# The first expert's rows by a one-hot product instead of a gather, in a hybrid decoder layer with a mixture of experts

## The reference, cut to what matters

```python
h = rms_norm(x, norm_ffn[l]) * (1 + sc2) + sh2
x = x + g2 * hier_moe(h, ...)

def hier_moe(h, w_rg, b_rg, w_re, b_re, w_gate, w_up, w_down):
    ...
    for gi in range(N_EXPERT_GROUPS):
        hid = silu(einsum('nd,edf->nef', t, w_gate[gi])) * einsum('nd,edf->nef', t, w_up[gi])
        y = y + einsum('nef,efd->nd', hid * combine[:, gi, :, None], w_down[gi])
```

## Time and profile before

| | |
|---|---|
| Median of 3 runs | 785.83 us (782.81 to 786.27) |
| The profiled execution: own time, span of its trace | 787.4 us, 785.7 us |
| Mean granted TensorE clock | 0.941 of full speed |
| Busy in the span: PE, DVE, ACT, POOL | 681.1, 317.3, 180.1, 117.9 us |
| Moved by DMA | 174.13 MB, mean 222 GB/s |

### The profile page before, as it was taken

How to read it: one execution, slowest core, us unless ns; L and a number is a source line. 1 busy time by engine, 2 the same in 40 slices (tenths; PEclk the granted TensorE clock), 3 DMA queues, 4 the chain that set the end, 5 groups by cost and what they waited for, 6 DMA issues and landing times.

```text
span 785.7 us, 9804 instructions
## 1 busy us (share of the span) xinstructions
PE 681.1 (87%) x3799; PEld 396.2 (50%) x3803; DVE 317.3 (40%) x749; ACT 180.1 (23%) x434; POOL 117.9 (15%) x165
## 2 busy tenths in 40 slices
PE   1799999999999998889999953999999999999820
PEld 1674446667675796555544443444544544443300
DVE  3204757757576443766522245350211211212117
ACT  3205224031120212556511140120211211201103
POOL 8700124123050273000000001010000000000030
PEclk9999999999999999989999975899999999999975
DMA  9999003973330302640161077438999999999964
GB/s 329 375 261 362 2 0 108 300 236 108 108 108 1 55 2 104 181 201 1 67 202 54 28 304 311 161 105 357 370 424 411 403 410 407 390 406 414 415 205 181
DMA packets 73826, 174.13 MB, mean 222 GB/s; under 512 B 21970, under 2 KB 38956, under 8 KB 69932
## 3 DMA queue, kind: packets, MB, share of 16 engines
q1 hardware_dynamic: 67728, 157.59, 55.1%
q0 software_dynamic: 2816, 9.96, 3.6%
q10 hardware_dynamic: 3228, 5.84, 2.0%
HBM read 157.12 MB, written 16.26 MB: 221 GB/s over the span
## 4 chain that ended last, share of the span: by engine, by line
PE 74%; DVE 8%; DMA 7%; POOL 4%; ACT 3%; issue 3%; POOLq 0%; ACTq 0%; SPq 0%; DVEq 0%
PE ps L1025 14%; PE ps L1141 7%; PE ps L2281 7%; PE ps L1058 6%; PE ps L2248 5%; DMA gu<-in_w_up 4%; PE ps L1019 4%; PE ps L2359 2%; PE ps L2365 2%; PE ps L2245 2%; PE ps L1053 2%; PE ps L2272 2%; POOL lev L1629 2%; PE ps L653 2%; PE ps L2369 2%
## 5 line engine op out<-in xcount | busy, mean ns | idle before, releaser
L1025 PE MATMUL ps<-gu,xgT 128*128 128x512 f32 x256 | 114.1, 605 | 2.8 <-ACT xgT L1068 2.8
L1025 PEld LDWEIGHTS ps<-gu,xgT 128*128 128x128 f32 x256 | 49.1, 194 | 63.3 <-issue 63.3
L1521 POOL DMA_INDIRECT xg<-xn_rows,list x16 | 14.9, 930 | 390.7 <-PE ps L994 182.6
L2281 PE MATMUL ps<-hT,winr 128*128 128x512 f32 x144 | 72.6, 612 | 0.2
L1141 PE MATMUL ps<-wout,yT 128*128 128x512 f32 x128 | 57.6, 609 | 0.0
L1058 PE MATMUL ps<-dn,hidT 128*128 128x512 f32 x128 | 56.5, 594 | 0.0
L1734 POOL TENSOR_TENSOR cc<-low,lev 128x512 f32<-128x512 f32 x20 | 30.2, 1520 | 129.5 <-DVE low L2068 104.0
L1872 DVE SCALAR_TENSOR_TENSOR acc<-ada,st,acc 128x512 f32<-128x512 f32 x56 | 48.5, 867 | 1.3
L1019 PE MATMUL ps<-gu,xgT 128*32 128x256 f32 (+1 forms) x384 | 43.0, 452 | 1.1 <-DMA gu<-in_w_up 1.1
L2248 PE MATMUL ps<-hT,wind 128*128 128x512 f32 x96 | 42.3, 593 | 0.0
L1141 PEld LDWEIGHTS ps<-wout,yT 128*128 128x128 f32 x128 | 24.6, 195 | 30.0 <-issue 30.0
(11 more groups left out here) (429 smaller groups left out, 1041.4 us busy)
## 6 DMA issues: line engine op xcount, KB each, us to landing
dn<-in_w_down SPq DMA_DIRECT2D x16, 2048.0 KB, 23.5
gu<-in_w_gate SPq DMA_DIRECT2D x15, 2048.0 KB, 22.2
gu<-in_w_up SPq DMA_DIRECT2D x15, 2048.0 KB, 26.7
ada<-in_w_ada SPq DMA_DIRECT2D x12, 2048.0 KB, 11.7
expert_rows<-zero SPq DMA_DIRECT2D x12, 512.0 KB, 7.0
expert_rows<-yo ACTq DMA_DIRECT2D x8, 512.0 KB
wout<-in_w_out SPq DMA_DIRECT2D x1, 3072.0 KB, 10.4
x<-in_x SPq DMA_DIRECT2D x2, 1024.0 KB, 6.4
```

The lines of the kernel that those rows point to most:

```text
L1025: ins = nc.tensor.matmul(PS[2 * b + w][:, :], T["xgT"][:, k, :], w_in[:, w, k, :], start=(k == 0), stop=(k == KT - 1))
L2281: ins = t.matmul(bank[:, :], w(k), T["hT"][:, k, :], start=(k == 0), stop=(k == KT - 1))
```

## The change

Gather 0, its list and its transposes go. In their place PE multiplies x2 itself (stationary, 128 tokens x 128 features) with the one-hot matrix of expert 0 (moving, 128 tokens x 128 rows), summed over the four token tiles, for each of the eight feature steps: 32 matmuls whose results in PS[6] and PS[7] are already transposed rows. `rstd2` is folded into the one-hot matrix, which is now made by four instructions of 128 x 128 instead of one of 128 x 512. As the features are in the natural order now, the first expert's gate and up are loaded as `(k p) f -> p k f`, and its scale and shift are `A2` and `mod` directly. The waits of the later transposes for their gathers are counted one lower on the even tiles, which share `xg[0]`. The rank products move from PS[6] to PS[4]. ACT starts on its half after the fourth feature step (`first_half`). Expert 1's list product comes after the 32 matmuls on PE, and its copy (and so gather 1) behind `dve_rows(0)` on DVE.

```diff
+    first_v = [A[n][0].rearrange("g e (k p) f -> (g e) p k f", p=P)[0] for n in ("w_gate", "w_up")]
...
-        load_gate_up(sp, 0, 0)
+        for w, view in enumerate(first_v):
+            sp.dma_start(gu[0][:, w], view).then_inc(sem("gu_in0"), 16)
...
     def act_rows(act, n):
-        act.wait_ge(sem("mod_moved"), 48)
-        act.wait_ge(sem("xg_tr"), n + 1)
+        if n:
+            act.wait_ge(sem("mod_moved"), 48)
+            act.wait_ge(sem("xg_tr"), n + 1)
+        else:
+            act.wait_ge(sem("first_half"), 1)
+        scale, shift = (rA, rshift) if n else (A2, mod[:, 24:32])
...
-        rank = PS[6][:, 0:(ST + 1) * E]
+        rank = PS[4][:, 0:(ST + 1) * E]
...
-        for e in range(2):
-            pe.wait_ge(sem("routing"), ROUTING[("first_rows", "second_rows")[e]])
+        pe.wait_ge(sem("routing"), ROUTING["first_rows"])
+        for k in range(KT):
             for i in range(ST):
-                ins = t.matmul(PS[4 + e][:, 0:1], T["in_row"][:, e, i, :], T["tok"][:, i:i + 1], start=(i == 0),
-                               stop=(i == ST - 1))
-            ins.then_inc(sem("routing_pe"), 1)
-
-        pe_rows(pe, 0, 0, 16)
+                ins = t.matmul(PS[6 + k // 4][:, (k % 4) * P:(k % 4 + 1) * P], T["x2"][:, i, k * P:(k + 1) * P],
+                               T["in_row"][:, 0, i, :], start=(i == 0), stop=(i == ST - 1))
+            if k == 3:
+                ins.then_inc(sem("first_half"), 1)
+        ins.then_inc(sem("xg_tr"), 1)
+        pe.wait_ge(sem("routing"), ROUTING["second_rows"])
+        for i in range(ST):
+            ins = t.matmul(PS[5][:, 0:1], T["in_row"][:, 1, i, :], T["tok"][:, i:i + 1], start=(i == 0),
+                           stop=(i == ST - 1))
+        ins.then_inc(sem("routing_pe"), 1)
         pe_gate_up(pe, 0, 0)
...
-        for e in range(2):
-            v.scalar_tensor_tensor(T["in_row"][:, e], T["row_n"][:].unsqueeze(1).broadcast_to([P, ST, P]), 1.0,
-                                   r16[:, :, e:e + 1].broadcast_to([P, ST, P]), ALU.add,
-                                   ALU.is_equal).then_inc(sem("routing"), 1)
+        link(v.tensor_scalar(r16, r16, -1.0, None, ALU.add))
+        for i in range(ST):
+            ins = v.tensor_scalar(T["in_row"][:, 0, i, :], T["row_n"][:], r16[:, i, 0:1], rstd2[:, i:i + 1],
+                                  ALU.is_equal, ALU.mult)
+        ins.then_inc(sem("routing"), 1)
+        v.tensor_tensor(T["in_row"][:, 1], T["row_n"][:].unsqueeze(1).broadcast_to([P, ST, P]),
+                        r16[:, :, 1:2].broadcast_to([P, ST, P]), ALU.is_equal).then_inc(sem("routing"), 1)
...
-        dve.wait_ge(sem("routing_pe"), ROUTING_PE["first_list_mm"])
-        v.tensor_copy(T["list"][:, 0:1], PS[4][:, 0:1]).then_inc(sem("routing"), 1)
-        dve.wait_ge(sem("routing_pe"), ROUTING_PE["second_list_mm"])
-        v.tensor_copy(T["list"][:, 1:2], PS[5][:, 0:1]).then_inc(sem("routing"), 1)
...
         dve_rows(dve, 0)
+        dve.wait_ge(sem("routing_pe"), ROUTING_PE["second_list_mm"])
+        v.tensor_copy(T["list"][:, 1:2], PS[5][:, 0:1]).then_inc(sem("routing"), 1)
...
-        pool.wait_ge(sem("routing"), ROUTING["first_list"])
...
-        for n in range(E):
+        for n in range(1, E):
```

More of the change, by code:

```diff
@@ L50 @@
 NBUF = 3
-ROUTING = {"before_tile": 1, "first_rows": 2, "second_rows": 3, "first_list": 4, "second_list": 5, "experts": 6,
-           "places": 7, "list": 8, "w12": 9, "slots": 10, "route_i": 11}
-ROUTING_PE = {"rank_mm": 1, "first_list_mm": 2, "second_list_mm": 3, "list_mm": 4}
+ROUTING = {"before_tile": 1, "first_rows": 2, "second_rows": 3, "experts": 4, "second_list": 5,
+           "places": 6, "list": 7, "w12": 8, "slots": 9, "route_i": 10}
+ROUTING_PE = {"rank_mm": 1, "second_list_mm": 2, "list_mm": 3}
 SIZES = [128] * 8 + [64] * 4 + [32] * 4
@@ L1068, in act_rows @@
             ins = nc.scalar.activation(T["xgT"][:, k, 0:m], PS[6][:, k * m:(k + 1) * m], ACT.Identity,
-                                       scale=rA[:, k:k + 1], bias=rshift[:, k:k + 1])
+                                       scale=scale[:, k:k + 1], bias=shift[:, k:k + 1])
         ins.then_inc(sem("xgT_a"), 1)
@@ L1093, in dve_rows @@
     def dve_rows(dve, n):
-        dve.wait_ge(sem("mod_moved"), 48)
+        if n:
+            dve.wait_ge(sem("mod_moved"), 48)
+        scale, shift = (rA, rshift) if n else (A2, mod[:, 24:32])
         dve.wait_ge(sem("xg_tr"), n + 1)
@@ L1097, in dve_rows @@
         for k in range(4, KT):
-            ins = nc.vector.tensor_scalar(T["xgT"][:, k, 0:m], PS[7][:, (k - 4) * m:(k - 3) * m], rA[:, k:k + 1],
-                                          rshift[:, k:k + 1], ALU.mult, ALU.add)
+            ins = nc.vector.tensor_scalar(T["xgT"][:, k, 0:m], PS[7][:, (k - 4) * m:(k - 3) * m], scale[:, k:k + 1],
+                                          shift[:, k:k + 1], ALU.mult, ALU.add)
         ins.then_inc(sem("xgT_d"), 1)
@@ L1220, in pe_moe @@
             if n + 1 < E:
-                pe_rows(pe, n + 1, 1 - b, 16 * ((n + 1) // 2 + 1))
+                pe_rows(pe, n + 1, 1 - b, 16 * ((n + 2) // 2))
             if n == 1:
@@ L1228, in extra @@
         def extra(x, n):
-            pe_rows(pe, n, 0, 16 * (E // 2 + x + 1))
+            pe_rows(pe, n, 0, 16 * (E // 2 + x))
             pe_gate_up(pe, n, 0)
@@ L1365, in dve_moe @@
         rank, cnt, xe, t16, incl, bb = (T[n][:] for n in ("rank", "count", "xe", "t16", "incl", "bb"))
-        link(v.tensor_copy(rank, PS[6][:, 0:ST * E].rearrange("p (i e) -> p i e", i=ST)))
+        link(v.tensor_copy(rank, PS[4][:, 0:ST * E].rearrange("p (i e) -> p i e", i=ST)))
         r16 = T["r16"][:]
         link(v.scalar_tensor_tensor(r16, rank, 1.0, T["chosen"][:, 0:ST], ALU.add, ALU.mult))
-        for e in range(2):
-            v.scalar_tensor_tensor(T["in_row"][:, e], T["row_n"][:].unsqueeze(1).broadcast_to([P, ST, P]), 1.0,
-                                   r16[:, :, e:e + 1].broadcast_to([P, ST, P]), ALU.add,
-                                   ALU.is_equal).then_inc(sem("routing"), 1)
-        link(v.tensor_copy(cnt, PS[6][:, ST * E:(ST + 1) * E]))
+        link(v.tensor_scalar(r16, r16, -1.0, None, ALU.add))
[5 more added lines that the diff above has]
+                        r16[:, :, 1:2].broadcast_to([P, ST, P]), ALU.is_equal).then_inc(sem("routing"), 1)
+        link(v.tensor_copy(cnt, PS[4][:, ST * E:(ST + 1) * E]))
         key, versus, order, pad, tile0 = (T[n][:] for n in ("key", "versus", "size", "pad", "tile0"))
```

## The result

Over 13 runs each the changed kernel has a median of 782.23 us and the kernel before 786.73 us. One run of the changed kernel was disturbed (1758 us) and is left out of the ratio. The ratio is 0.9934, with a 95% interval of 0.9914 to 0.9955: of 786.73 us that is 5.2 us less, between 3.5 and 6.8 (the medians themselves differ by 4.5). The forecast was 777.6 us and 8.2 us less, with a range of 775.2 to 781.5. The direction was right, the size was not.

A forecast was written before the change was run, and what follows sets the result against it. The prediction took the chain through gather 0 to the first gate-up, at half clock, as the bound, with PE releasing the later loads. 5.9 + 3.0 - 0.7 = 8.2 us, so 785.83 becomes 777.6 us, range 775.2 to 781.5.

The forecast's parts named there:

- The bound: Routing to end: PE releases each weight load, so an earlier first gate-up moves loads, both bounds and tail equally.
- The start of the first gate-up: After the routing: DVE's chain and `dve_rows(0)` come last, so the start moves from 492.85 to 487.0, 5.9 us.
- the pause: Before the first gate-up: 1 to 3 us with only PE's narrow list product; clock fall 4 in 10, 0.7 us.
- gather 1 was hidden: Expert 1's rows: issued about 488, landing 491.6 to 500.1, needed at 502.4; hidden by 2.3 us at worst.
- The clock: First gate-up: PE comes warm from the products, 13.73 instead of 16.75 us, 3.0 us gained, less 0.7 for a fall.
- a pause that costs the whole 3.0: Rival before the first gate-up: the clock gain is lost, 779.9 us; 0.09 together with a chain 1.5 us longer.
- Half clock throughout: Rival in the one-hot products: they don't raise the clock, gate-up starts at 490.7, gain 2.15, 783.7 us; chance 0.06.
- an unmoved end: Rival from 550 us on: DMA is the bound and doesn't move, so the end stays at 785.8 us; chance 0.05.
- a late gather: Rival at tile 1: gather 1 as slow as the slowest load, rows at 519.7, total 794.2 us; chance 0.04.

The follow-up runs named there:

- a_look1: The changed kernel without edit, one single profiled execution: stage 29.83 us, first gate-up 15.67 us, span 776.5 us.
- a_oldload: The changed kernel with expert 0's gate and up loaded as before, in runs of 16 KB: ratio 0.9943 to the kernel before.
- a_extra: The changed kernel with one more gather, of expert 1's rows, ahead of gather 1: ratio 0.9931 to the kernel before.
- a_look6: The changed kernel without edit, another single profiled execution: stage 28.12 us, first gate-up 13.97 us, span 777.8 us.
- the repeat: The changed kernel timed again without edit: ratio 0.9929 to the kernel before; in its profile a stage of 29.84 us.

## Why the prediction was right or wrong

**The bound, right.** The gather's place on the chain was the cost, the loads started earlier with PE, and the gain of the stage reaches the end. Three other versions show it too: 10.7 us less in the stage than the mean of the kernel before (25.48 for 36.15) came out as 9.9 us (0.9874, so 7.5 to 12.3), 12.2 (23.96) as 12.3 (10.1 to 14.5), and 3.0 (33.14) as 3.1 (0.6 to 5.7). Each stage is from one profile, so that they agree so closely is in part luck.

**The start of the first gate-up, right.** Forecast 5.9 us earlier; over the profiles it is 14.17 us after the rank copy instead of 20.02, so 5.85. `dve_rows(0)` starts 12.65 us after the rank copy in the first profile (490.81); the text had 485.5 - 472.82 = 12.68. The products took 8.94 to 10.09 us, where the text's bounds were 9.3 to 10.4 us, the pause was there, and gather 1 was hidden.

**The clock, wrong, and this is the step that failed.** The text took "13.73 instead of 16.75: 3.0 us" and gave a fall of the clock in the pause 4 in 10 at 1.7 us, so 2.3 on average. Measured are 16.13 and 15.43 on average: **0.7 us**. The mechanism was named rightly, and the price of a fall too (15.67 - 13.97 = 1.7 us); three sizes were off. The clock fell at the pause in 7 of 8 profiles, not in 4 of 10, which takes 0.8 us. The 16.75 of the first profile is the highest of six, where the others are 15.87 to 16.07, so 0.6 us too high for the mean; I took one profile's value for something that depends on where a dip of the clock happens to end. And the first gate-up at full clock takes 13.97 us, not the 13.73 of a later tile, 0.2 us more. With 0.7 in place of 2.3 the sum is 6.55, the difference of the two stages in the table, which lies inside the measured interval (3.5 to 6.8). What lies between 6.5 and the measured 5.2 is not explained.

On the rule that I weighed: the Trainium skill (TensorE: Matmul & The Clock Gate, the HAM clock gate) ties the fall to an idle TensorE and would have left the pause harmless. The trace was right to be preferred: in the first profile the engine worked 0.90 of 2.3 us around the pause, and the clock fell. I trusted the row too little and gave it 4 in 10. Where exactly the fall comes varies: within 0.3 us of the start of the first gate-up in six profiles, 1.2 us behind it in a_look1. Of the ten profiles with an unfilled pause (a_oldload and a_extra included) the two without a fall, a_look6 and a_oldload, are those in which the clock had risen 6.4 us after the rank copy, and not at 5.1 or at 7.2 to 7.6. By these ten the fall seems to hang on when the clock rose; why is open.

**What is not closed.** The profiles don't add up to the medians exactly. Their mean spans differ by 784.55 - 777.5 = 7.05 us, made of 6.55 in the stage and 1.3 behind it, less 0.8 ahead of it; the two timed comparisons give 5.2 and 5.6, with intervals up to 6.8 and 7.7. In the first profile of the changed kernel and in the repeat, the two that belong to timed comparisons, the rank copy was 5.3 and 4.0 us later than in the kernel before; in the other six it wasn't. So it is shown that single executions scatter by such amounts ahead of the routing, and that at equal dips the change costs nothing there. Whether the timed runs of the changed kernel had more of it, and why, is open. The 1.3 us behind the stage are open as well: over the profiles of the table the last load takes 31.34 instead of 31.72 us on average, and the last gathers 6.11 instead of 6.82, together 1.1; one gather more didn't bring that back.

The rival that came nearest is "a pause that costs the whole 3.0", which I had at 779.9 with 0.09; the measured 5.2 us below 785.83 would be 780.6. Half clock throughout, an unmoved end and a late gather didn't happen. One sum of the prediction is off: the lower end of the range, 785.83 - 8.9 - 1.5, is 775.4 and not 775.2, which changes nothing here. By the repeated medians the base moved as well: 786.73 instead of 785.83, 0.9 of the 4.6 us between forecast and result.

## What to carry to other kernels

A gather on the critical chain of 12 us can be replaced by a one-hot product of rows that are still on chip, and the next bound is then whatever ran under its cover: here DVE's chain, 12.6 us long. Look at once whether the consumer needs all of its input; letting PE start on ACT's half gave nearly as much again (0.9874 instead of 0.9929, about 4 us, from six runs) for three lines. Never book a gain of TensorE's clock from one profile: compare several of the same kernel, and where the trace of before shows a fall while the engine is partly at work, take a fall in a new pause as likely, though not as certain: it came in 8 of 10 profiles here, and not in a pause of 1.70 us in the kernel before with a warm PE.

## What the runs showed of the hardware that was not expected

The clock fell at a pause of 1.4 to 2.5 us, and stayed at half for some 3.2 us under full load, in 7 of 8 executions. Feeding TensorE with useless products before it is needed paid in the kernel before (3.1 us, between 0.6 and 5.7), and in the version on ACT's half it shortened the one-hot products from 8.94 to 7.41 us; there the ratio went from 0.9874 to 0.9844, within the noise of the two. And two executions of the same kernel can differ by 5 us ahead of the routing, with the clock's dips at other places and of other lengths, while the rank copy came within 0.01 us where the dips agreed (474.75 and 474.76).
